# The samples' dots as one multiply-and-sum per head, and the head work of the last input step inside its unit

## What is computed

```
q, k, v, qi, ki, wi = split(a @ w_in);  q = rope(q);  k = rope(k)
idx   = top 64 keys of each query by the indexer
# prompt: 256 queries of 8 heads, 128 wide; samples: 8 queries, keys gathered from paged caches
logits = sum_d q[h, d] * k_sel[key, h, d] * 128 ** -0.5
p      = softmax(logits);  o = sum_key p * v_sel
h      = h + o @ w_out
```

## Time and profile before

| | |
|---|---|
| median of 3 runs | 625.97 us (625.36 to 627.49) |
| the profiled execution | 626.0 us |
| its span in the profile | 624.1 us |
| mean granted TensorE clock | 0.989 |
| busy share: PE, DVE, ACT, POOL | 95%, 74%, 59%, 38% |

### The profile page before, as it was taken

How to read it: one execution, slowest core, us unless ns; L and a number is a source line. 1 busy time by engine, 2 the same in 40 slices (tenths; PEclk the granted TensorE clock), 3 DMA queues, 4 the chain that set the end, 5 groups by cost and what they waited for, 6 DMA issues and landing times.

```text
span 624.1 us, 12833 instructions
## 1 busy us (share of the span) xinstructions
PE 594.3 (95%) x5081; PEld 512.0 (82%) x5081; DVE 461.8 (74%) x844; ACT 366.4 (59%) x620; POOL 238.0 (38%) x259
## 2 busy tenths in 40 slices
PE   7989986989999999999999989998999999999995
PEld 6878875878888888888888878886888888888885
DVE  4779998555788877778678786888777888785442
ACT  6784454555776655666555679456755665653322
POOL 4222343742335444552000399913444544420000
PEclk9999998989999999999999999998999999999998
DMA  9768594233967666677997852045666666779501
GB/s 262 198 168 217 156 339 138 72 99 94 314 195 210 198 192 193 197 224 221 263 269 219 232 168 71 1 120 156 189 194 188 202 199 193 227 215 241 151 6 69
DMA packets 205420, 113.28 MB, mean 182 GB/s; under 512 B 5561, under 2 KB 202217, under 8 KB 205337
## 3 DMA queue, kind: packets, MB, share of 16 engines
q1 hardware_dynamic: 203169, 106.33, 60.5%
q0 software_dynamic: 1680, 5.79, 2.7%
q10 hardware_dynamic: 512, 0.35, 0.2%
HBM read 108.83 MB, written 3.86 MB: 181 GB/s over the span
## 4 chain that ended last, share of the span: by engine, by line
PE 66%; DVE 18%; ACT 5%; issue 4%; DMA 3%; POOL 2%; SPq 1%; DVEq 0%; POOLq 0%; ACTq 0%
PE acc L1419 18%; PE acc L1425 18%; PE acc L1422 18%; DVE w_lo L935 6%; DMA stage<-in_w_ffn_down 2%; ACT w_hi L589 2%; PE acc L1431 1%; DVE area L1065 1%; PE acc L1559 1%; PE acc L1561 1%; PE acc L1560 1%; PE misc L1742 1%; DVE aL L944 1%; DVE area L935 1%; DVE qk L1068 1%
## 5 line engine op out<-in xcount | busy, mean ns | idle before, releaser
L1419 PE MATMUL acc<-aH,w_hi 128*128 128x264 f16 (+1 forms) x904 | 250.9, 278 | 2.3 <-DVE aL L944 2.0
L1422 PE MATMUL acc<-aL,w_hi 128*128 128x264 f16 (+1 forms) x904 | 250.7, 277 | 0.0
L1425 PE MATMUL acc<-aH,w_lo 128*128 128x264 f16 (+1 forms) x904 | 250.5, 277 | 0.0
L935 DVE SCALAR_TENSOR_TENSOR w_lo<-stage,w_hi 128x1024 f16<-128x1024 f32 (+1 forms) x155 | 203.9, 1319 | 36.9 <-ACT w_hi L589 36.6
L589 ACT ACTIVATE w_hi<-stage 128x1024 f16<-128x1024 f32 (+1 forms) x155 | 171.6, 1109 | 40.5 <-PE acc L1425 27.5
L1419 PE MATMUL acc<-zH,w_hi 128*128 128x264 f16 x384 | 106.0, 276 | 0.0
L1425 PE MATMUL acc<-zH,w_lo 128*128 128x264 f16 x384 | 106.0, 276 | 0.0
L1422 PE MATMUL acc<-zL,w_hi 128*128 128x264 f16 x384 | 106.0, 276 | 0.0
L1419 PEld LDWEIGHTS acc<-aH,w_hi 128*128 128x128 f16 (+1 forms) x904 | 89.1, 99 | 17.5 <-DVE aL L944 2.5
L1422 PEld LDWEIGHTS acc<-aL,w_hi 128*128 128x128 f16 (+1 forms) x904 | 90.4, 100 | 14.1 <-issue 0.3
L1425 PEld LDWEIGHTS acc<-aH,w_lo 128*128 128x128 f16 (+1 forms) x904 | 90.4, 100 | 13.4
(11 more groups left out here) (405 smaller groups left out, 971.9 us busy)
## 6 DMA issues: line engine op xcount, KB each, us to landing
stage<-in_w_ffn_up SPq DMA_DIRECT2D x88, 512.0 KB, 4.5
stage<-in_w_ffn_down SPq DMA_DIRECT2D x32, 704.0 KB, 5.9
stage<-in_w_attn_in SPq DMA_DIRECT2D x22, 512.0 KB, 7.0
stage<-in_w_rec_in SPq DMA_DIRECT2D x16, 512.0 KB, 4.9
stage<-in_w_attn_out SPq DMA_DIRECT2D x8, 512.0 KB, 3.8
stage<-in_w_rec_out SPq DMA_DIRECT2D x8, 512.0 KB, 3.8
area<-in_w_attn_in SPq DMA_DIRECT2D x4, 512.0 KB, 5.3
area<-in_x_prompt SPq DMA_DIRECT2D x2, 512.0 KB, 4.8
```

What stands on the lines that cost most here:

```text
L935: v.scalar_tensor_tensor(low, stage[:, place_in_line(u) % 4, 0:n, 0:cols], WSCALE, high, ALU.mult, ALU.subtract).then_inc(lo_done, 1)
L1419: t_.matmul(out, high[:, c, :], xH[:, x0 + c, :], start=first and c == 0, stop=False)
L1422: t_.matmul(out, high[:, c, :], xL[:, x0 + c, :], start=False, stop=False)
L1425: ins = t_.matmul(out, low[:, c, :], xH[:, x0 + c, :], start=False, stop=last and c == n - 1)
```

## The change

`sample_dots` no longer multiplies 1024 features in one instruction and sums them in another: for each of the 8 heads one `tensor_tensor_reduce` multiplies 128 features and sums them, with one wait behind the eighth. In the steps from 22 on ScalarE's order changes: exp of the samples' logits goes behind the copy of the turned key and the half swap. In step 26 (`INSIDE`) TensorE runs the head work between the matmuls of unit 26, after the 11th; ScalarE runs the head work of step 27 before it keeps unit 26's values; VectorE makes the low half of head 0 ahead of the coefficients' first part, and the logits and the low half that stood in step 27 ahead of the second part; the split of unit 30 goes to step 27, behind the coefficients and the samples' halves, on ScalarE and VectorE.

```diff
+INSIDE = 26
 # ScalarE
+            def after_heads(u):
+                for n, (at, _, _) in enumerate(TURNS):
+                    if at == u - 1:
+                        keep_turned(n)
+                if u == INSIDE + 1:
+                    o_high(u - LG - 5)
+                if LG + 3 <= u < LG + 3 + H:
+                    keep_pT(u - LG - 3)
+                if LG + 5 <= u and u != INSIDE + 1:
+                    o_high(u - LG - 5)
...
+                if u == 23:
+                    act.wait_ge(prm_ready, 1)
+                    nc.scalar.activation(spl[:, 1, :], spl[:, 0, :], ACT.Exp, scale=-1.0).then_inc(sp_exp, 1)
+                if u != INSIDE + 1:
+                    after_heads(u)
+                if u < U_OUT and u not in U_V:
+                    swap_halves(u)
                 if u == 22:
                     act.wait_ge(smx_done, 1)
                     nc.scalar.activation(sl[:], sl[:], ACT.Exp).then_inc(sexp_done, 1)
...
+                if u == INSIDE:
+                    after_heads(u + 1)
                 if u in U_V:
                     keep_v(u)
-                if u != 27:
+                if u not in (INSIDE, INSIDE + 1):
                     for x in splits_of_step(u):
                         hi(x)
...
-                    for x in splits_of_step(u):
+                    for x in splits_of_step(INSIDE) + splits_of_step(INSIDE + 1):
                         hi(x)
 # VectorE
-                steps.done(v.tensor_tensor(kgat[:, j, :].rearrange("p (t d) -> p t d", t=2), qb,
-                                           kgat[:, j, :].rearrange("p (t d) -> p t d", t=2), ALU.mult))
-                steps.wait()
-                steps.done(v.tensor_reduce(qk[:, j, :], kgat[:, j, :].rearrange("p (h d) -> p h d", h=H), AX.X, ALU.add))
-                steps.wait()
+                for h in range(H):
+                    key = kgat[:, j, h * P:(h + 1) * P]
+                    ins = v.tensor_tensor_reduce(key, key, qb[:, h // 4, h % 4 * P:(h % 4 + 1) * P], 1.0, 0.0, ALU.mult, ALU.add,
+                                                 qk[:, j, h:h + 1])
+                small(ins)
...
+                if u == INSIDE:
+                    o_low(u - LG - 5)
                 if u == 26:
...
+                if u == INSIDE:
+                    logits(u - LG)
+                    o_low(u - LG - 4)
...
+                for x in [] if u == INSIDE else splits_of_step(INSIDE) + splits_of_step(u) if u == INSIDE + 1 else splits_of_step(u):
                     lo(x)
 # TensorE
+                    elif u == INSIDE:
+                        between = lambda i: heads_of_step(INSIDE) if i == 7 else None
...
+                if u != INSIDE:
+                    heads_of_step(u)
```

18 lines of the change are left out of this document (2 added, 16 removed).

## The result

The changed kernel takes **621.89 us** (median of 8 runs, 620.41 to 624.73); the kernel before, beside it, takes 626.07 us (8 runs, 624.29 to 627.49). The ratio is 0.9936, with a 95% interval of 0.9912 to 0.9959. The profiled execution takes 621.39 us, its span is 619.5 us and its mean granted clock 0.989. The forecast was 621.5 in a range of 619.4 to 624.1.

What follows compares the result with a forecast made beforehand. VectorE was taken to bound the rounds of the samples' dots. 626.0 less 4.3 (dots and step 22) and 1.6 (last step) gave 620.1; plus 1.4 for a clock fall, 621.5 us, range 619.4 to 624.1.

Steps and rivals of the forecast that it cites:

- the dots' part: VectorE's four rounds of sample dots: 0.205 us a head, rounds of 4.25 for 5.01, first logits 3.0 us earlier.
- The 0.53 beside GpSimd: Dots' rounds: the 0.53 us VectorE's multiply loses beside GpSimd's subtraction stays, once per round.
- half throughput: Rival in the dots: by the page's rule 0.34 us a head, rounds 0.3 longer, 624.5 us in all, chance 0.10.
- Transfers: Rival in the dots' rounds: unit 23's load comes some 3 us late, half of part 1 goes, 623.0 us, chance 0.07.
- 1.6 us to spare: Third-party margin in the rounds: unit 23's split can't start before 92.6 us; VectorE wants it at 94.2.
- Step 22: Samples' softmax on ScalarE behind key 3's copy and the half swap: logits of head 1 0.7 us earlier beyond the dots.
- 0.5 more: Step after 22: logits of head 2 follow those of head 1 by 4.75 us in place of 5.3, 0.5 gained.
- part 1 and 2: Dots' rounds (part 1, 3.0 us) and ScalarE's order in step 22 (part 2, 0.7 and 0.5): sum 4.3 us.
- Last step: Unit 26's start to the projection's second head block: 11.0 us in place of 12.55, 1.6 gained, bounds 0 to 2.3.
- the waits of 0.7, 0.9 and 0.6: Around the projection's first chunk: three waits of 0.5 to 1.1 us, one of 0.7 on unit 30's split.
- One fall at the price of 1.4: Clock falls once inside unit 23, behind the new 2.6 us wait at head 1's logits: 1.4 lost, 621.5 us, chance 0.41.

Runs made afterwards that it cites:

- key 0 run: Changed kernel with key 0's copy on ScalarE ahead of unit 23's high half and three sample coefficients moved earlier on VectorE: 622.63 us, ratio to before 0.9942.
- idle matmuls: Changed kernel with three coefficients moved earlier and matmuls that compute nothing in TensorE's waits of steps 20 (11) and 22 (9): 621.88 us, ratio to before 0.9917.
- scale on ScalarE: Changed kernel with three coefficients moved earlier and the dots' scale taken from VectorE to ScalarE, behind key 1's copy: 623.77 us, ratio to before 0.9963.

## Why the prediction was right

The time fell where it was forecast, to 0.4 us, and the dots' part is right in mechanism and size. That the whole is so close is luck in part. By the ratios the dots give 2.6 us (0.9959), step 22 on top of them 1.2 more (0.9939), and the last step 0.2 (0.9936); the intervals reach 1.5 to 1.8 us to either side. The forecast had 4.3 for the first two and 1.6 for the last, and took 1.4 off for the clock. The last step's gain doesn't show in the runs, though their spread doesn't exclude it, and the clock's price was not paid where it was forecast; in the sum the two nearly cancel.

**Dots: right.** Forecast 0.205 a head, a round of 4.25 and 3.0 us in all; measured 0.212, 4.32 and 2.76, the same to 0.02 in eight traces. The 0.53 beside GpSimd stands as forecast (0.76 against 0.21). Page and trace differ: the Trainium skill, "Vector Engine (DVE) Microarchitecture Reference", section "7. Points that are easy to get wrong", has half throughput for this kind of instruction with two SBUF sources that aren't bf16; every trace of the new dots without a wait per head has 128 float32 columns in 0.21 us, both sources in SBUF. The measurement decides. The trace calls the instruction CUSTOM_DVE_ANT_0, and no run shows whether the page means that one; the weight split, a SCALAR_TENSOR_TENSOR with both sources in SBUF and neither bf16, does 1024 columns in 1.13 us, which isn't half rate either.

**Transfers: half right.** "1.6 us to spare" was true of VectorE's split, which never waited. I did not ask who else is queued behind ScalarE's wait: key 0's copy is, and through it TensorE stood 2.62 us. It cost the rounds nothing, as the key 0 run shows, and in six of nine traces with a wait of 2.1 us or more at this place the clock is low behind it.

**Step 22: right in its price, wrong in its order of effects.** 0.6 to 0.8 us by the start of head 1's logits (forecast 0.7), with dots and without. The "0.5 more" in the next step came only where the clock stayed full: the logits of head 2 follow those of head 1 by 4.74 us with idle matmuls (forecast 4.75) and by 4.89 with scale on ScalarE, by 5.2 to 6.1 in the other traces of after's order with the new dots. There the early fall makes unit 22 late (in two of them a second fall adds to it), and with it the half swap, the softmax's table load (102.50 to 103.78 in after) with the exp behind it (until 104.4, past the start of head 1's logits at 103.95) and the split behind that. So part 1 and 2 together are 3.4 us in place of 4.3 in the first trace of after, 2.6 in the second.

**Last step: right in the trace, not seen in the runs.** 11.15 us against a forecast of 11.0, with the waits of 0.7, 0.9 and 0.6 where they were forecast. By the forecast all of the 1.6 us gained is low clock (1.7), and the traces bear that out: where the clock doesn't fall, the old order is as fast. But the forecast took it that what is removed here is won for the program. Over the runs the edit doesn't raise the mean granted clock: 0.9877 against before's 0.9873 alone, 0.9892 against 0.9893 beside the other two edits. One stretch of 3.4 us less would be 3.4 x 0.5 / 622 = 0.0027 more, and the standard error of either difference is 0.0009. Where the low clock stands instead is open.

**The clock: right by chance.** One fall at the price of 1.4, behind the wait at head 1's logits, made the step from 620.1 to 621.5. In the profiled execution it was not there; it was in two of the four traces that have this code up to 118 us, and those are 0.6 to 0.9 us behind the other two there, so the price is about half of the 1.4. What filled its place in the sum were the 0.9 us short in parts 1 and 2 and a late fall: TensorE waits 2.1 us ahead of the recurrent layer's output projection (362 us), and in six of the fourteen traces, this one among them, the clock falls behind that. It loses 1.7 us between 355 and 375 us; some 1.0 of it is made good elsewhere behind 141 us, which leaves the 0.7 of "later". The sum of the trace is 3.4 + 1.4 - 0.7 = 4.1, and 0.5 us by which this execution was ahead before the change's place.

Over all runs of each kernel, before has a median of 625.97 us (111 runs) and after 622.0 (20 runs).

**What stays open.** The length of a wait sorts the traces only roughly. Ahead of key 3's turn or head 1's logits the clock fell behind 3.1 to 3.3 us (three traces), 2.75, 2.58 and 2.21, and not behind 2.42 (scale on ScalarE), 2.05 and 1.82; behind the 2.43 to 2.46 in step 27 in four of five traces; and behind waits of 2.1 to 2.9 at 92 to 93 us in six of nine. Why dots with step 22 are better than dots alone by more than the 0.8 us of the order, and why scale on ScalarE shows its microsecond in the trace and not in the median, the mean granted clocks of the runs answer in part: 0.9893 against 0.9865 in the first pair, 0.9873 with scale on ScalarE against 0.9892 in after. They don't say in which wait the clock fell, and each of these differences is only 1.5 to 2.2 of its standard errors.

## What to carry to other kernels

Where the tensor engine waits for others over some stretch, an edit has two prices: what it saves on the bounding engine, which one trace tells to a few hundredths, and where it puts the low clock, which changes from run to run. An edit that only breaks up a wait is worth what the clock would have cost, and nothing where it would not have fallen; here, alone, it left the median where it was. Read the granted clock of every timed run beside that of the profiled one, which may be a lucky one. Ask of each low stretch whether the engine has slack there: in the rounds it costs nothing, and one pair of traces (before and the last step alone) suggests that without it the engine stands longer in one piece and the low stretch falls on the path. Matmuls that compute nothing, put into two such waits, raised the mean clock of the runs from 0.988 to 0.993.

## What was not expected of the hardware

- A multiply-and-sum of 128 float32 columns with both sources in SBUF starts the next one 0.212 us later, its sum's read (0.08) inside; with a wait for itself 0.333. The reads don't add up.
- The instruction that stands beside GpSimd's subtraction of 264 columns loses 0.55 us and ends as the subtraction does (the next head starts at 87.16, the subtraction ends at 87.09). The one multiply of 1024 columns that stood there before, with 0.68 us of the subtraction beside it, lost 0.53, so splitting it in eight costs nothing more. What eight such instructions under a longer one would lose, no run here shows.
- The granted clock is low for 3.4 us in some traces and for 10 us in two, at nearly the same wait (3.33 us with dots alone, 3.11 and 3.32 in the two kernels with the last step's edit). In both long ones it fell 1.0 us or more before the wait ended (103.5 against 104.48, 105.4 against 106.65), in dots alone 0.2 us before (104.3 against 104.54). The Trainium skill, "TensorE: Matmul & The Clock Gate", section "Part 1: The HAM clock gate (the "warmup" mystery)", says of the low clock at a kernel's start that how many matmuls meet it varies from run to run of the same kernel; the two traces of after show the same in the middle of one: 1.00 from 102 to 108 us in the first, 0.72 in the second.
- The load of unit 23 lands at 91.5 us in before and at 91.4 in after, though VectorE runs ahead in after. The DMA share is 1.05 and 1.06 from 80 to 90 us, so the traffic of the gathers may be what bounds it; no run here separates it from the load's issue.
